# Order of TensorE work in a mixture-of-experts loop: halves of the last gate-up tiles, gathers and combination moved

## The reference

```
logits = t @ w_router + b_router;  top_v, top_e = top_k(logits, 4);  gate = softmax(top_v)
per expert e, for its tokens x:  gu = x @ w_gate_up[e] + b_gate_up[e]          # 1024 -> 2048
    glu = min(gu[:, :1024], 7);  lin = clip(gu[:, 1024:], -7, 7)
    act = glu * sigmoid(1.702 * glu) * (lin + 1)
    y += gate * (act @ w_down[e] + b_down[e])                                  # 1024 -> 1024
x += gate2 * RMSNorm_post2(y)
```

## Time and profile before

| | us |
|---|---|
| median of 3 runs | 1408.66 (1406.51 to 1409.88) |
| profiled execution, own time | 1412.01 |
| its span, first to last instruction | 1410.2 |
| PE busy | 1337.6 |
| DVE busy | 342.4 |
| ACT busy | 223.2 |
| chain that ended last: PE 55%, DMA 40%, DVE 2% | |
| bytes moved | 486.89 MB |

### The profile page before, as it was taken

The page is one execution under the profiler, slowest core; times in us unless marked ns, Lnnn a source line. Parts: engine busy times, 40 slices in busy tenths (PEclk is TensorE's granted clock), DMA queues, the critical chain, the costliest instruction groups (busy, mean ns, idle before and its releaser), DMA issues.

```text
span 1410.2 us, 15800 instructions
## 1 busy us (share of the span) xinstructions
PE 1337.6 (95%) x6279; PEld 616.2 (44%) x6279; DVE 342.4 (24%) x727; ACT 223.2 (16%) x455; POOL 25.8 (2%) x56
## 2 busy tenths in 40 slices
PE   5999999999999999999999999999999999999996
PEld 2666666665454334343343433434334343343432
DVE  2643325631334201022010220101211022110123
ACT  2113304432422101011010110111001011010102
POOL 1100000010001000000000000000000000000000
PEclk9999999999979999999999999999999999999998
DMA  9846483463365999999999999999999999999992
GB/s 351 262 163 260 160 284 119 172 247 119 120 223 207 382 417 427 427 429 427 426 429 426 429 427 428 420 422 427 429 428 422 429 420 428 422 428 425 428 426 96
DMA packets 63264, 486.89 MB, mean 345 GB/s; under 512 B 10349, under 2 KB 15205, under 8 KB 35540
## 3 DMA queue, kind: packets, MB, share of 16 engines
q1 hardware_dynamic: 61508, 480.85, 82.9%
q0 software_dynamic: 1680, 4.91, 1.1%
HBM read 481.63 MB, written 4.12 MB: 344 GB/s over the span
## 4 chain that ended last, share of the span: by engine, by line
PE 55%; DMA 40%; DVE 2%; issue 1%; SPq 1%; ACT 1%; DVEq 0%; ACTq 0%
DMA ring<-in_w_gate_up_dram 38%; PE bank L1894 22%; PE bank L1496 10%; PE bank L1525 5%; PE bank L1381 2%; PE bank L1692 2%; PE bank L1882 2%; DMA ring<-in_w_in_dram 1%; PE bank L1448 1%; PE bank L1643 1%; PE bank L1885 1%; PE bank L1858 1%; SPq L447 1%; PE bank L1618 1%; DMA ring<-in_w_ada_dram 1%
## 5 line engine op out<-in xcount | busy, mean ns | idle before, releaser
L1894 PE MATMUL bank<-ring,work 128*64 128x512 f32 x2048 | 452.2, 595 | 17.9 <-DMA ring<-in_w_gate_up_dram 8.8
L1894 PEld LDWEIGHTS bank<-ring,work 128*64 128x64 f32 x2048 | 162.2, 137 | 293.0 <-issue 293.0
L1894 PE MATMUL bank<-ring,hT 128*64 128x512 f32 x1024 | 230.3, 596 | 15.4 <-DMA ring<-in_w_gate_up_dram 15.4
L1357 DVE TENSOR_TENSOR gbT<-gbT,bank 128x512 f32<-128x512 f32 x85 | 58.5, 688 | 458.3 <-PE bank L1885 321.9
L1894 PEld LDWEIGHTS bank<-ring,hT 128*64 128x64 f32 x1024 | 78.0, 137 | 164.8 <-issue 164.8
L1496 PE MATMUL bank<-hT,ring 128*128 128x320 f32 x512 | 142.0, 438 | 2.1 <-DMA ring<-in_w_in_dram 2.1
L1496 PEld LDWEIGHTS bank<-hT,ring 128*128 128x128 f32 x512 | 97.5, 192 | 47.5 <-issue 8.8
L1325 DVE TENSOR_SCALAR work<-bank 128x512 f32<-128x512 f32 x32 | 22.0, 686 | 316.1 <-PE bank L1894 316.1
L782 ACT ACTIVATE work<-bank 128x320 f32<-128x320 f32 x16 | 7.0, 437 | 423.3 <-PE bank L1381 423.3
L1525 PE MATMUL bank<-hT,ring 128*128 128x320 f32 x256 | 73.4, 436 | 0.2 <-ACT gaT L609 0.2
L1858 PE MATMUL bank<-qT,tok 128*128 128x256 f32 x256 | 72.4, 405 | 0.0
(11 more groups left out here) (347 smaller groups left out, 828.5 us busy)
## 6 DMA issues: line engine op xcount, KB each, us to landing
ring<-in_w_gate_up_dram SPq DMA_DIRECT2D x128, 2048.0 KB, 16.1
ring<-in_w_down_dram SPq DMA_DIRECT2D x64, 2048.0 KB, 17.1
ring<-in_w_ada_dram SPq DMA_DIRECT2D x12, 2048.0 KB, 10.4
ring<-in_w_in_dram SPq DMA_DIRECT2D x12, 2048.0 KB, 11.1
ring<-in_cache_k_dram SPq DMA_DIRECT2D x16, 512.0 KB, 5.4
ring<-in_cache_v_dram SPq DMA_DIRECT2D x16, 512.0 KB, 4.4
ring<-in_w_out_dram SPq DMA_DIRECT2D x2, 2048.0 KB, 9.2
out_dram<-tok POOLq DMA_DIRECT2D x2, 1024.0 KB, 5.8
```

The lines of the kernel that those rows point to most:

```text
L1357: TTo(piece(gbf, i), piece(gbf, i), B[6 + n % 2][:, :], ALU.add).then_inc(s["scatter_read"], 1)
L1894: last = mm(bank[CAP * x:CAP * x + CAP, :], lhsT[:, CAP * x:CAP * x + CAP], rhs(x), start=start, stop=stop)
```

## The change

- The gate-up steps 6 and 7 are done by column halves: first the glu tile 0 and linear tile 2 of both steps, then tiles 1 and 3. `used` rises after each half instead of each step. DVE waits for half 0 only before its first clips, and finishes the activation of half 0 before it turns to half 1.
- Behind the gate-up: one gather, turn of half 0, one gather, down steps 0 and 1, turn of half 1, down steps 2 to 7, then the other two gathers. They go through B[6] and B[7] instead of B[4] and B[5].
- ACT copies in the matching order: turned half 0, first `XT` copy, turned half 1, the two `Y` copies, second `XT` copy.
- The combination pieces stand behind steps 2, 3 and 4 instead of 0, 1 and 2, and wait also for the second `XT` copy of the pair before.
- The waits for `XT` at the start of a pair are split: the first step waits for one copy fewer, and the last copy is awaited at the third column tile of step 0 (`u` = 0) or at step 6 (`u` = 2).

```
# ACT
+            def XT_out(buf, half, i, n):
+                eng.wait_ge(s["gather_ps"], n)
+                m = 4 * half + 2 * i
+                A_(XT[buf][:, m:m + 2, :], B[6 + i][:, :]..., ACT.Copy).then_inc(s["XT_made"], 1)
...
+                turned_out(0)
+                XT_out(1 - u // 2, u % 2, 0, 2 * t + 5)
+                turned_out(1)
                 eng.wait_ge(s["used"], 16 * t + 32)
                 for j in range(2):
                     A_(Ysb[:, 512 * j:512 * j + 512], B[4 + j][:, :], ACT.Copy).then_inc(s["Y_made"], 1)
+                XT_out(1 - u // 2, u % 2, 1, 2 * t + 6)
# DVE
-                eng.wait_ge(s["used"], 16 * t + 24)
                 def clip_glu(j):
+                    eng.wait_ge(s["used"], 16 * t + (23, 24)[j])
...
                 clip_glu(0)
                 clip_lin(0)
+                gated(0)
+                act(0)
                 clip_glu(1)
-                gated(0)
                 clip_lin(1)
-                act(0)
                 gated(1)
                 act(1)
# PE
                     if n == 0:
                         eng.wait_ge(s["C_made"], t + 1)
                         eng.wait_ge(s["Y_made"], 2 * t + 1)
+                        eng.wait_ge(s["XT_made"], 2 * t + 4)
...
                 for k in range(NT):
                     if k == 0:
-                        eng.wait_ge(s["XT_made"], ready + 2)
+                        eng.wait_ge(s["XT_made"], 2 * t + (3 if u % 2 == 0 else 2))
+                    if k == 6 and u == 2:
+                        eng.wait_ge(s["XT_made"], 2 * t + 4)
...
+                    if k < 6:
+                        for j in range(4):
+                            if k == 0 and u == 0 and j == 2:
+                                eng.wait_ge(s["XT_made"], 2 * t + 4)
+                            last = gate_up(k, j)
+                        last.then_inc(s["used"], 1)
+                    if k == 6:
+                        for h in range(2):
+                            for j in (h, 2 + h):
+                                gate_up(6, j)
+                                last = gate_up(7, j)
+                            last.then_inc(s["used"], 1)
+                    if k in (2, 3, 4):
+                        combine(t, ((0, 1), (2, 3), (4,))[k - 2])
...
-                gather(u % 2, 4)
-                for j in range(2):
-                    (turn of half j)
-                eng.wait_ge(s["XT_made"], 2 * t + 6)
+                gather(u % 2, 0)
+                act_turned(0)
+                gather(u % 2, 1)
                 for k in range(NT):
+                    if k == 2:
+                        act_turned(1)
...
+                eng.wait_ge(s["C_made"], t + 2)
+                gather(u % 2, 2)
+                gather(u % 2, 3)
```

More of the change, by code:

```diff
@@ L766, in _ @@
             A_(tope[:, 2, 0:TOPK], tope[:, 2, 0:TOPK], ACT.Exp).then_inc(s["topexp_made"], 1)
[L769 to L774, removed]
+            def XT_out(buf, half, i, n):
+                eng.wait_ge(s["gather_ps"], n)
+                m = 4 * half + 2 * i
+                A_(XT[buf][:, m:m + 2, :], B[6 + i][:, :].rearrange("p (t s) -> p t s", t=2), ACT.Copy).then_inc(s["XT_made"], 1)
             for i, (m, bank) in enumerate(((0, 0), (4, 6), (2, 1), (6, 2))):
@@ L782, in pair, with turned_out @@
                 A_(C, B[7][0:SL, 0:T], ACT.Copy).then_inc(s["C_made"], 1)
+                def turned_out(j):
+                    eng.wait_ge(s["aT_ps"], 2 * t + (j + 1))
+                    A_(actT[:, 4 * j:4 * j + 4, :], B[j][:, 0:4 * SL].rearrange("p (t s) -> p t s", t=4), ACT.Copy)\
+                        .then_inc(s["aT_made"], 1)
                 for j in range(2):
@@ L786, in pair @@
                         .then_inc(s["sig_made"], 1)
-                XT_out(1 - u // 2, u % 2, 2 * t + 5, 4)
-                for j in range(2):
-                    eng.wait_ge(s["aT_ps"], 2 * t + (j + 1))
-                    A_(actT[:, 4 * j:4 * j + 4, :], B[j][:, 0:4 * SL].rearrange("p (t s) -> p t s", t=4), ACT.Copy)\
-                        .then_inc(s["aT_made"], 1)
+                turned_out(0)
+                XT_out(1 - u // 2, u % 2, 0, 2 * t + 5)
+                turned_out(1)
                 eng.wait_ge(s["used"], 16 * t + 32)
@@ L1851, in _, with gather @@
                         last.then_inc(s["gather_ps"], 1)
[L1853 to L1861, removed]
+            def gather(half, i):
+                m, q = 4 * half + i, 64 * half
+                out = B[6 + i // 2][:, QUAD * (i % 2):QUAD * (i % 2) + QUAD]
+                for k in range(2):
+                    mm(out, tok[:, k, 128 * m:128 * m + 128], sel[:, k, :], start=(k == 0), stop=False)
+                last = mm(out, tok[q:q + 64, 2, 128 * i:128 * i + 128], sel[q:q + 64, 2, :], start=False, stop=True)
+                if i % 2:
+                    last.then_inc(s["gather_ps"], 1)
             eng.wait_ge(s["wtok_made"], 2)
@@ L1898, in pair, with gate_up, act_turned @@
                 slots = XT[u // 2][:, :, SL * (u % 2):SL * (u % 2) + SL]
-                ready = 2 * t + (2 if u % 2 == 0 else 0)
+                def gate_up(k, j):
+                    return both(B[j], slots[:, k, :], lambda x: gu_slot[k - k % 2 + x][:, k % 2, 512 * j:512 * j + 512],
+                                k == 0, k == NT - 1)
+                def act_turned(j):
+                    eng.wait_ge(s["act_made"], 2 * t + (j + 1))
+                    for m in range(4):
+                        last = tr(B[j][:, SL * m:SL * m + SL], glu[:, half_columns(j, m)], 128)
+                    last.then_inc(s["aT_ps"], 1)
                 for k in range(NT):
                     if k == 0:
-                        eng.wait_ge(s["XT_made"], ready + 2)
+                        eng.wait_ge(s["XT_made"], 2 * t + (3 if u % 2 == 0 else 2))
+                    if k == 6 and u == 2:
+                        eng.wait_ge(s["XT_made"], 2 * t + 4)
                     if k % 2 == 0:
```

## The result

The changed kernel is slower: 1413.43 us against 1408.49 in the first comparison (6 runs each), ratio 1.0027 with a 95% interval of 1.0018 to 1.0037, and 1412.69 against 1409.52 in a second one (r_after), ratio 1.0026 (1.0014 to 1.0038). The medians differ by 4.9 and 3.2 us; the ratios, which use all runs, make it 3.7 to 3.8 us lost. A gain of 2.75 was forecast.

A forecast was written before the change was run, and what follows sets the result against it. The weight stream was taken as the bound, 58.7 us a pair. Against the profiled execution, -3.9 + 1.3 - 3.3 + 3.0 + 0.15 = -2.75; applied to the 1408.66 us median this gave 1405.9 us, range 1401.8 to 1409.8.

The forecast's parts named there:

- The stream starts earlier: Pair 0: weight loads held back by TensorE are issued sooner, so the stream is 3.9 us earlier from pair 1 on.
- the three causes: In pair 0: first held-back load 2.4 us earlier, hole behind the fourth step closed (0.8), half-way hole of down projection shortened (0.7).
- The middle gains nothing, the last gate-up ends 1.3 later: Steady pairs stay at 58.7 us; the moved combination makes gate-up 1.2 to 1.3 us later, shown only in the last pair.
- Down end -3.3: Last pair: the down projection ends 18.8 us behind the gate-up instead of 22.1, 3.3 us less.
- The end, +3.0 and +0.15: Behind the last down projection: gathers and copy delay the combination by 3.0 us, DVE's weighing and selection add 0.15.
- DVE is in the same trap: Last pair: DVE's unused weighing and selection wait for the last gather, ending 0.1 to 0.2 us after the piece is ready.
- Neither sign: Forecast wrong if a steady pair takes other than 58.7 us, or if TensorE waits for DVE or ACT at a turn.
- (a): Weight stream: a deeper queue removes pauses of about 1.6 us; 1402.7 us without two, 1399.5 without all four; chance 0.18.
- (b): Weight stream: the rate rises with a fuller queue and TensorE bounds, down to 1385 us; chance 0.02.
- (c): Weight stream: slot release and landing form a loop, the head start is lost; 1408.7 to 1409.8 us; chance 0.13.
- (d): Expert pairs: TensorE becomes the bound through new stalls, from 1.5 us a pair; about 1415 us at 2; chance 0.12.
- (e): First turn: DVE and ACT finish the first half no earlier, the turn waits 2 us; 1407.9 us; chance 0.07.

The follow-up runs named there:

- r_after_2: The changed kernel again, unchanged, for a third trace; 949.9 us from the expert stage's start to the last add.
- r_after_3: The changed kernel again, unchanged, for a fourth trace; 952.2 us from the expert stage's start to the last add.
- e_comb_only: The kernel before with one part alone, the combination behind steps 2, 3 and 4; ratio to the kernel before 1.0007.
- e_comb_134: Changed kernel, last gathers between down steps 3 and 4, second XT copy before Y copies, combination behind steps 1, 3, 4; 0.9989, again 0.9981 against the kernel before.
- e_late_gathers_only: Changed kernel with whole gate-up steps, combination behind 0, 1, 2 and DVE's old order, keeping two gathers behind the down projection; ratio to the kernel before 1.0003.
- e_filled: Changed kernel, last gathers between down steps 3 and 4, second XT copy before Y copies, three unread products before each third gate-up step; 1.0149 against the kernel before.
- r_before: The kernel before once more, unchanged, against itself; ratio 0.9999.
- e_changed_134: The changed kernel with the combination behind steps 1, 3 and 4, two gathers still behind the down projection; ratio to the kernel before 1.0012.

## Why the prediction was wrong

By its own steps, from the stage's start:

- **The stream starts earlier, -3.9.** Right. The weights of the last pair's third step come, against the stage's start, 3.9, 3.4, 4.6 and 3.3 us earlier than in the trace of before (changed, r_after, r_after_2, r_after_3). That the three causes hang together was not seen: without the shorter way to the half-way mark, the first two are worth 0.8 (e_comb_only). With pieces 0 and 1 behind step 1 and the shorter way to that mark the start is 2.4 and 2.1 us earlier (e_comb_134, e_comb_134_again).
- **The middle gains nothing, the last gate-up ends 1.3 later.** Right: 37.8 us behind the landing of the pair's first weights, 36.6 before (39.6 in r_after, with the fall of the clock). The 58.7 us a pair stayed. The Trainium skill (DMA: Bandwidth & Descriptors, Where 436 GB/s comes from) gives 435 GB/s for the ports; the traces stay below it, with 428 GB/s in a full pair of the changed kernel.
- **Down end -3.3.** Right: 18.6 instead of 22.2, -3.5.
- **The end, +3.0 and +0.15.** This is the step that failed. "DVE is in the same trap" named the place, but counted only the two ops, "0.1 to 0.2 after the first combined piece could be taken", and then "What follows is as before". What stood there: the two ops, then 3.1 to 3.2 us of way out of the loop on DVE, then six rows of products at a half clock, 1.5 us more than at the full one. From down end to last add it is 8.0 us more than before instead of 3.15, so the sum is +2.0 where it was -2.75. The 8.0 can be taken apart. e_late_gathers_only, with the short way out, has 4.2: 1.0 more than the 3.15, because even the short way out has its place behind the two ops. Another 2.3 is what DVE's new order adds to the way out, and 1.5 is the clock, which held where PE stood 0.99 us and fell where it stood 2.6 to 3.3 us. The first of these could have been read before: the trace of before shows 0.74 us from DVE's last op to the instruction behind the branch. The longer way out could not: it came with the edit, and no run shows why DVE's new order brings it.

Neither sign that the prediction had named for itself appeared: the steady pair took 58.7 us, and PE waited for nothing at a turn. They watched the loop, and the loss lay behind it.

The sum of +2.0 is below the first measured interval (2.5 to 5.2 us) and at the edge of the second (2.0 to 5.4); the traces average +2.5, the ratios say 3.7. What remains, 1 to 2 us, has no step of its own. Falls of the clock in the last pair carry some of it (1.7 to 2.2 us in one trace of four); that they carry all isn't shown.

The rivals: (a) is out, the slips of 1.6 us are there in the same number (four in the changed trace too) although the queue was longer. (b) is out by the rate. (c) holds for the combination alone, by another mechanism: the head start is lost at the next hole, not in a loop of latencies. (d) is borne out in its arithmetic by e_filled and out for this change. (e) is out: the turn waited for nothing. None of them held the loss, and the chance of 0.12 for slower stood for (d) alone.

The better version: the halves, the shorter way to the down projection and pieces 0 and 1 behind step 1 are worth 1.5 to 2.7 us, if the gathers stand between down steps 3 and 4: 0.9989 and 0.9981 in two comparisons, the second alone beyond its interval. That the place of the pieces adds to it isn't shown: with them behind steps 0, 1 and 2 it was 0.9991.

## What to carry to other kernels

When work is moved behind the last product of a loop, follow each engine from there to the first instruction behind the loop: way out, table loads and register reads come onto the path with it. Read their price from the sequencer's rows even where it is covered, and don't take it as fixed: here an edit that seemed free by itself raised it from 0.74 to 3.1 us. When the bound is a stream of loads, write down for each issue how long its queue is; an earlier issue is worth only what the next late one leaves of it. And compare stages between traces, not spans: here untouched code ahead of the stage moved by 9 us from one execution to the next.

## What the runs showed of the hardware

- Behind the same skipping branch, DVE's next instruction came after 0.52 to 0.53 us in four traces of three programs and after 2.8 to 3.1 in thirteen traces of nine programs, whose DVE lists differ in order and by one register instruction a pair.
- Within the stage the TensorE clock fell from its upper level of 2.4 GHz to 1.2 for 3.4 us at a time (twice 6.8), in most places behind idle times of 2.0 to 3.9 us, but no idle time decides it by itself. In the changed trace it held behind 2.10 us at 1041.48 and fell behind 2.10 us at 863.73. Before, it held behind 2.19 and 2.49 us at the loop edges; in r_before it fell behind 2.47 and 2.05. At a loop edge it fell behind 1.54 us in e_changed_134 and 1.64 us in r_after_2, and in e_late_gathers_only three times at turns where PE had stood only 0.4 and 0.58 us for DVE. Behind the 1.82 us in the last pair of the changed trace it held.
- With one product of 0.96 us in that idle time of every pair the median granted clock rose from 0.982 to 0.986, with no measurable time won, since weights were awaited.
